# Rotary rows of all attention heads gathered in one tile, in a three-layer model kernel on one core

## The chip, the core and the metric

The kernel runs on one core of one Trainium2 chip. The metric is the device time of one execution in microseconds (us), the median over runs. A core has TensorE (PE in the profile), VectorE (DVE), ScalarE (ACT), GpSimd (POOL) and SyncE (SP), each with its own instruction queue, and 16 DMA engines. SP and ACT issue DMAs here. The engines wait for one another by semaphores alone.

## The reference

Two equal hybrid layers over 512 tokens of width 1024, then a third of another kind. Only the hybrid layer is touched:

```python
def apply_partial_rope(t, cos, sin):            # t: (B, S, 8 heads, 64)
    half = ROPE_DIM // 2                         # 8; ROPE_DIM = 16
    t1 = t[..., :half]
    t2 = t[..., half:ROPE_DIM]
    return jnp.concatenate([t1 * cos - t2 * sin, t2 * cos + t1 * sin, t[..., ROPE_DIM:]], axis=-1)

    h = rms_norm(x, norm_mix_w)
    z = h @ w_in + b_in
    aq, ak, av = ...                             # 8 heads of 64 each, from z
    aq = apply_partial_rope(aq, cos, sin)
    ak = apply_partial_rope(ak, cos, sin)
    ya = dilated_mixture_attention(aq, ak, av)
    yb = ...                                     # mLSTM branch
    x = x + (ga * (ya @ w_proj_att) + gb * (yb @ w_proj_mlstm)) @ w_out
    x = x + jnp.square(jax.nn.relu(rms_norm(x, norm_mlp_w) @ w_ff1)) @ w_ff2
```

So of the 64 rows of a head, 16 are turned and 48 pass through.

## The kernel before

Everything is fp32. A matrix product is three matmuls of split operands (`h_hi` with `w_hi`, `h_lo` with `w_hi`, `h_hi` with `w_lo`), 128x512 each. Activations lie feature-major: the queries and keys of a layer are one tile `qk` of 128 partitions and 8 x 512 columns; a block of 512 columns (one t) holds two heads, on partitions 0 to 63 and 64 to 127, blocks 0 to 3 the queries and 4 to 7 the keys. The rows that turn are partitions 0 to 15 and 64 to 79.

**The weight stream.** Weights come in units of 2048 columns (1 MB). Unit n is loaded by SP into `w_raw` (two slots), copied to `w_hi` by ACT (128x2048), and its remainder written to `w_lo` by POOL in four instructions of 128x512 (L297). SP issues the load of unit n once POOL has split unit n-2, because they share a slot. A unit of the input projection holds 48 matmuls.

**What sets the order.** Each engine's program is the concatenation of stages in one order. While a stage (`rope`, `att`, ...) waits on vector work, PE is given pieces of the input projection (`side`), six matmuls each. A stage gets a budget of pieces in `BESIDE1`: `rope` 18, `att` 36. In `rope` PE does nothing but its pieces. The first score matmul of `att` then waits for `rope.ends`. In `att` the pieces are spread over 19 steps.

**Units of a hybrid layer**, counted from 0: 0 to 3 give `qk`, 4 and 5 the values, 6 to 9 the input of the convolution (`conv_in`). The evacuation of `qk` is one DVE multiplication by `rstd` (L2972) and an ACT bias (L2976). Four units later (`LATER`), just behind the load of units 4 to 7, SP copies the 8-row halves of two blocks crosswise from `qk` to `rope_swapped` (`Rope.move`), so that the last such copies stand behind the load of unit 7. `rope_swapped` has the shape of `qk` and is otherwise zero (a memset by DVE, one for each of the two layers); `cos` is 1 and `sin` 0 in the rows that don't turn (`C_MSK`, `C_UNM`). `Rope.dve` rotates two blocks at a time with three 128x1024 operations, 12 in all, and multiplies the queries by -1/8 on the way.

Of the kernel before, what the change touches and what calls it, by code (L numbers as in the profile page):

```python
# [34 lines left out]
ALU = mybir.AluOpType  # L35
# [50 lines left out]
C_INV = C_PAT + TT * P  # L86
C_MSK, C_UNM = C_INV + 1, C_INV + 2
C_CNT = C_INV + 3
C_SEL = C_CNT + len(WINDOWS) * 16
# [7 lines left out]
def constants():  # L97
    c = np.zeros((P, C_END), np.float32)
    i = np.arange(P)
    c[:, C_ID:C_ID + P] = np.eye(P)  # L100
    c[:, C_ONE:C_ONE + 8] = 1.0
    c[:, C_QK:C_QK + P] = np.where(i[None, :] > i[:, None], BIG, 0.0)
    c[:, C_ST:C_ST + P] = np.where(i[:, None] > i[None, :], BIG, 0.0)
    c[:, C_KEEP:C_KEEP + P] = i[:, None] <= i[None, :]
    for b in range(TT):
        dist = i[:, None] - i[None, :] + (TT - 1 - b) * P
        n = sum(((dist >= 0) & (dist % dil == 0) & (dist <= win)).astype(int) for win, dil in PATTERNS)
        c[:, C_PAT + b * P:C_PAT + (b + 1) * P] = np.where(n > 0, -np.log(np.maximum(n, 1)), BIG)
    d = i % HD
    inv = np.float32(ROPE_THETA) ** (-np.arange(0, ROPE_DIM, 2, dtype=np.float32) / np.float32(ROPE_DIM))  # L110
    half = ROPE_DIM // 2
    c[:, C_INV] = np.where(d < ROPE_DIM, np.where(d < half, -inv[d % half], inv[d % half]), 0.0)
    c[:, C_MSK] = d < ROPE_DIM
    c[:, C_UNM] = d >= ROPE_DIM
    for g, w in enumerate(WINDOWS):
        c[:, C_CNT + 16 * g:C_CNT + 16 * (g + 1)] = 1.0 / np.minimum(np.arange(1, 17), w)
    c[:, C_SEL:C_SEL + SH] = i[:, None] % GROUP == np.arange(SH)[None, :]
    return c


class Stage:
# [55 lines left out]
    def act(self, e): pass  # L177
# [445 lines left out]
class Jobs(Stage):  # L623
# [3 lines left out]

    PIECE, LATER = 6, 4

    def __init__(self, k, name, prev, hand, before):  # L630
        super().__init__(k, name, prev)
        self.units, self.jobs, self.pieces = [], [], []
        self.pos = {"pe": 0, "act": 0, "dve": 0}
        self.joined = set()
        self.early = self.posts = 0
        self.moves = {}
        self.marks, self.marked = [], 0
        self.narrow, self.scale_at = None, None
        self.hand, self.before, self.hooks = hand, before, {}
# [266 lines left out]
class Rope(Stage):  # L906
# [4 lines left out]

    def __init__(self, k, name, prev, qk, swapped):
        super().__init__(k, name, prev)
        self.qk, self.swapped = qk, swapped
        self.ends = [self.at("turned", self.UNITS)]

    def tally(self):
        return {"swapped": 64 * self.UNITS, "cos": self.UNITS, "sin": self.UNITS, "turned": self.UNITS}

    def move(self, j):  # L920
        half, w = ROPE_DIM // 2, slice(2 * j * T, (2 * j + 2) * T)

        def issue(sp):
            for h in (0, HD):
                sp.dma_start(self.swapped[h:h + half, w], self.qk[h + half:h + 2 * half, w])\
                   .then_inc(self.sem("swapped"), 16)
                sp.dma_start(self.swapped[h + half:h + 2 * half, w], self.qk[h:h + half, w])\
                   .then_inc(self.sem("swapped"), 16)
        return issue

    def pe(self, pe):
        self.side_pe(pe, 0, 1)

    def dve(self, dve):
        k = self.k
        self.join(dve)
        both = lambda x: x.unsqueeze(1).broadcast_to([P, 2, T])
        for j in range(self.UNITS):
            self.side_out("dve", dve, 3 * j, 3 * self.UNITS)
            scale = -HD ** -0.5 if j < self.UNITS // 2 else 1.0  # L940
            w = slice(2 * j * T, (2 * j + 2) * T)
            tiles, swapped = (x[:, w].rearrange("p (a b) -> p a b", b=T) for x in (self.qk, self.swapped))
            if j == 0:
                dve.wait_ge(*self.at("swapped", 64 * self.UNITS))
            dve.scalar_tensor_tensor(tiles, tiles, scale, both(k.cos[:, :]), ALU.mult, ALU.mult)\
               .then_inc(self.sem("cos"), 1)
            self.side_out("dve", dve, 3 * j + 1, 3 * self.UNITS)
            dve.scalar_tensor_tensor(swapped, swapped, scale, both(k.sin[:, :]), ALU.mult, ALU.mult)\
               .then_inc(self.sem("sin"), 1)
            self.side_out("dve", dve, 3 * j + 2, 3 * self.UNITS)  # L950
            dve.wait_ge(*self.at("cos", j + 1))
            dve.wait_ge(*self.at("sin", j + 1))
# [1053 lines left out]
class Params(Stage):  # L2006
# [3 lines left out]
    def __init__(self, k, name, sets, norm, at):  # L2010
        super().__init__(k, name, [])
        self.sets, self.norm = sets, norm
        self.prow = [k.at(f"{name}_rows{i}", at + i * P, P) for i in range(len(sets))]
        self.nrow = k.at(f"{name}_norm", at + len(sets) * P, P)
        self.ends = [self.at("cols", 1 + len(sets) + 2 + DEPTH)]

# [18 lines left out]
    def dve(self, dve):  # L2035
# [68 lines left out]
class Setup(Stage):  # L2104
# [131 lines left out]
class Rotary(Stage):  # L2236


    def __init__(self, k, name, prev, angles):
        super().__init__(k, name, prev)  # L2240
        self.rs, self.rc = angles.w[2], angles.w[3]
        self.ends = [self.at("cos", 1)]

    def act(self, act):
# [3 lines left out]
        act.activation(k.cos[:, :], self.rc[:, :], ACT.Sin).then_inc(self.sem("sines"), 1)  # L2248

    def dve(self, dve):  # L2250
        k = self.k
        dve.wait_ge(*self.at("sines", 2))
        dve.tensor_scalar(k.cos[:, :], k.cos[:, :], k.cst[:, C_MSK:C_MSK + 1], k.cst[:, C_UNM:C_UNM + 1],
                          ALU.mult, ALU.add).then_inc(self.sem("cos"), 1)

# [665 lines left out]
def first_layer(k, l, A, st, before, setup, angles, params):  # L2921
# [34 lines left out]
    fill = add(Fill, "fill", [(mv[:, :].rearrange("p (g d) -> p g d", d=MD + 1)[:, :, MD:MD + 1], 1.0),  # L2956
                              (cv3[:, :, 0:CONV - 1], 0.0)] + ([(swapped[:, :], 0.0)] if l else []), prev=[])
    w_in = A["w_in"]
# [15 lines left out]

    def biased(dst, c, bcol, move=None):
        job = scaled(dst, c, lambda act: act.activation(dst, dst, ACT.Identity, bias=k.col(c0 + bcol)))  # L2976
        job.move = move
        return job

# [30 lines left out]
    def gate_out(dve, cols):  # L3010
        for s, n in spread.ends:
# [3 lines left out]
            vb[:, 512:520].unsqueeze(1).broadcast_to([P, TT, 8]), ALU.add)  # L3015
    rope = Rope(k, "rope", [], qk, swapped)
    for j in range(4):
        qk_at = plain(AQ + j * UC, UC, [biased(qk[:, t * T:(t + 1) * T], t, B1 + t, rope.move(j) if t % 2 else None)
                                        for t in (2 * j, 2 * j + 1)])
    side.hooks = {1: [params.turn], 6: [hand.sums], 8: [hand.spread]} if l == 0 else \  # L3020
# [42 lines left out]
    rest = add(Rest, "to_rope", side, max(at, qkv_at), qk_at, prev=[])  # L3063
    rope.prev = [rest, setup, rotary] if l == 0 else [rest]
    rope.settle()
# [266 lines left out]
def program(nc, A, table, out):  # L3332
    with ExitStack() as ctx:
# [55 lines left out]
```

## Time and profile before

| | |
|---|---|
| median of 3 runs | 2417.63 us (2417.51 to 2417.8) |
| the profiled execution's own time | 2417.25 us |
| its span, first to last instruction | 2415.4 us |
| granted TensorE clock, mean | 0.999 |
| PE busy | 2389.6 us, 99% of the span |
| DVE, ACT, POOL busy | 1013.5, 847.4, 1099.3 us (42%, 35%, 46%) |
| DMA moved | 218.27 MB, mean 90 GB/s |

Times in the rows are us from the start of the span. A row in order of time gives start, duration, engine, line and operation, and in brackets how long the engine was idle before it and who ended that. "SPq" and "ACTq" rows are DMA issues. The two hybrid layers show the same pattern, the second 738.60 us after the first at the place of this change; the argument is told for the first.

### The profile page before, as it was taken

The numbers are of one execution on the slowest core, as the hardware profiler recorded it, in microseconds if no ns is written. First come the engines' busy times: TensorE is split into PE (matmuls) and PEld (weight loads), VectorE is DVE, ScalarE is ACT, GpSimd is POOL, SyncE is SP. The second block draws the span as 40 slices with busy tenths as digits, with TensorE's granted clock in tenths as the row PEclk, the third lists the DMA queues.
The fourth block names the chain that finished last, engine by engine and source line by source line (L and its number), as shares of the span: only waits on it lengthen the run. The fifth ranks groups of instructions, "written<-read, shape, count | busy, mean of one in ns | idle before, by whom it ended". The sixth has DMA issues, their size and how long they took to land.

```text
span 2415.4 us, 28668 instructions
## 1 busy us (share of the span) xinstructions
PE 2389.6 (99%) x11096; PEld 1926.8 (80%) x11096; DVE 1013.5 (42%) x1559; ACT 847.4 (35%) x1045; POOL 1099.3 (46%) x796
## 2 busy tenths in 40 slices
PE   8999999999999999999999999999999999999998
PEld 7767888888888767888888888778786788888887
DVE  7657553201203557554211203668595534222202
ACT  5355333322324255233321323442425233322213
POOL 4524355554544533345554544352342345455542
PEclk9999999999999999999999999999999999999999
DMA  5212232223223222222223232221221222322221
GB/s 184 91 53 88 71 103 92 100 88 104 88 104 98 90 70 88 80 94 88 93 99 104 87 105 89 89 73 59 77 88 53 81 99 88 104 91 100 89 103 69
DMA packets 168837, 218.27 MB, mean 90 GB/s; under 512 B 8044, under 2 KB 143148, under 8 KB 168484
## 3 DMA queue, kind: packets, MB, share of 16 engines
q1 hardware_dynamic: 165988, 211.38, 26.5%
q10 hardware_dynamic: 2752, 5.52, 0.7%
q8 instruction: 70, 1.15, 0.2%
q14 instruction: 27, 0.22, 0.0%
HBM read 213.24 MB, written 2.11 MB: 89 GB/s over the span
## 4 chain that ended last, share of the span: by engine, by line
issue 47%; POOL 32%; PE 20%; POOLq 0%; DMA 0%; ACT 0%; DVE 0%; SPq 0%
POOL w_lo L297 32%; PE ps L338 4%; PE ps L336 4%; PE ps L337 4%; PE ps L856 3%; PE ps L1951 2%; PE ps L1953 2%; PE ps L1949 2%; DMA w_raw<-in_w_in 0%; POOLq L308 0%; PE ps L356 0%; PE ps L326 0%; PE ps L362 0%; PE ps L329 0%; PE ps L325 0%
## 5 line engine op out<-in xcount | busy, mean ns | idle before, releaser
L297 POOL TENSOR_TENSOR w_lo<-w_raw,w_hi 128x512 fp32r<-128x512 f32 x792 | 1099.1, 1419 | 1289.6 <-ACT w_hi L283 1279.9
L283 ACT ACTIVATE w_hi<-w_raw 128x2048 fp32r<-128x2048 f32 x197 | 377.4, 1916 | 1044.8 <-PE ps L338 393.7
L856 PE MATMUL ps<-h_hi,w_hi 128*128 128x512 f32 x912 | 370.1, 406 | 4.5 <-POOL w_lo L297 2.9
L856 PE MATMUL ps<-h_hi,w_lo 128*128 128x512 f32 x912 | 356.5, 391 | 0.0
L856 PE MATMUL ps<-h_lo,w_hi 128*128 128x512 f32 x912 | 355.7, 390 | 0.0
L336 PE MATMUL ps<-h_hi,w_hi 128*128 128x512 f32 x816 | 319.4, 391 | 0.0
L338 PE MATMUL ps<-h_hi,w_lo 128*128 128x512 f32 x816 | 318.0, 390 | 0.0
L337 PE MATMUL ps<-h_lo,w_hi 128*128 128x512 f32 x816 | 317.8, 389 | 0.0
L856 PEld LDWEIGHTS ps<-h_hi,w_hi 128*128 128x128 f32 x912 | 171.5, 188 | 46.4 <-issue 8.2
L856 PEld LDWEIGHTS ps<-h_hi,w_lo 128*128 128x128 f32 x912 | 171.3, 188 | 37.0
L856 PEld LDWEIGHTS ps<-h_lo,w_hi 128*128 128x128 f32 x912 | 171.8, 188 | 35.8 <-issue 2.1
L1951 PE MATMUL ps<-ff_lo,w_hi 128*128 (+1 forms) x512 | 199.4, 390 | 0.0
L1953 PE MATMUL ps<-ff_hi,w_lo 128*128 (+1 forms) x512 | 199.4, 390 | 0.0
L1949 PE MATMUL ps<-ff_hi,w_hi 128*128 (+1 forms) x512 | 199.4, 389 | 0.0
L337 PEld LDWEIGHTS ps<-h_lo,w_hi 128*128 128x128 f32 x816 | 153.3, 188 | 32.5 <-issue 0.7
L336 PEld LDWEIGHTS ps<-h_hi,w_hi 128*128 128x128 f32 x816 | 153.3, 188 | 32.1 <-issue 0.7
L338 PEld LDWEIGHTS ps<-h_hi,w_lo 128*128 128x128 f32 x816 | 153.3, 188 | 31.7
L1999 DVE TENSOR_TENSOR xT<-xT,ps 128x512 f32<-128x512 f32 x40 | 27.5, 688 | 346.4 <-PE ps L1953 345.9
L1949 PEld LDWEIGHTS ps<-ff_hi,w_hi 128*128 128x128 f32 x512 | 96.2, 188 | 20.0
L1951 PEld LDWEIGHTS ps<-ff_lo,w_hi 128*128 128x128 f32 x512 | 96.2, 188 | 19.9
L1953 PEld LDWEIGHTS ps<-ff_hi,w_lo 128*128 128x128 f32 x512 | 96.2, 188 | 19.7
L1812 DVE SCALAR_TENSOR_TENSOR ff_relu<-ps,rstd 128x1024 f32<-128x1024 f32 x32 | 39.2, 1225 | 165.9 <-PE ps L338 157.9
(419 smaller groups left out, 3511.7 us busy)
## 6 DMA issues: line engine op xcount, KB each, us to landing
w_raw<-in_w_in SPq DMA_DIRECT2D x71, 1024.0 KB, 4.8
w_raw<-in_w_ff SPq DMA_DIRECT2D x64, 1024.0 KB, 5.1
w_raw<-in_w_ffn_in SPq DMA_DIRECT2D x22, 1024.0 KB, 4.9
w_raw<-in_w_out SPq DMA_DIRECT2D x12, 1024.0 KB, 5.1
w_raw<-in_w_ffn_out SPq DMA_DIRECT2D x11, 1024.0 KB, 4.7
w_raw<-in_w_proj_att SPq DMA_DIRECT2D x4, 1024.0 KB, 4.8
w_raw<-in_w_proj_mlstm SPq DMA_DIRECT2D x4, 1024.0 KB, 4.8
w_raw<-in_w_up_ssd SPq DMA_DIRECT2D x4, 1024.0 KB, 4.6
```

What stands on the lines that cost most here:

```text
L283: act.activation(k.whi[:, slot * SLOT:(slot + 1) * SLOT], k.wraw[:, slot * SLOT:(slot + 1) * SLOT], ACT.Copy).then_inc(k.hi_done, CHUNKS)
L297: pool.tensor_tensor(k.wlo[:, a:a + T], k.wraw[:, a:a + T], k.whi[:, a:a + T], ALU.subtract)\
L336: pe.matmul(out, k.whi[:, w], xh(i), start=i == 0, stop=False)
L337: pe.matmul(out, k.whi[:, w], xl(i), start=False, stop=False)
L338: mm = pe.matmul(out, k.wlo[:, w], xh(i), start=False, stop=i == kt - 1)
L856: mm = pe.matmul(out, lhs, rhs, start=i == 0 and n == 0, stop=stop and n == 2)
L1812: dve.scalar_tensor_tensor(r.rearrange("p (a b) -> p a b", b=T), k.ps[:, 2 * j:2 * j + 2, :], 0.0, rstd, ALU.max, ALU.mult).then_inc(self. ...
L1949: pe.matmul(k.ps[:, c, :], k.whi[:, w], self.fhi[:, x], start=first and i == 0, stop=False, skip_group_check=True)
L1951: pe.matmul(k.ps[:, c, :], k.whi[:, w], self.flo[:, x], start=False, stop=False, skip_group_check=True)
L1953: mm = pe.matmul(k.ps[:, c, :], k.wlo[:, w], self.fhi[:, x], start=False, stop=last and i == 1, skip_group_check=True)
L1999: dve.tensor_tensor(x, x, k.ps[:, c, :], ALU.add).then_inc(self.sem("added"), 1)
```

## The change

The rows that turn, 16 of each of 8 blocks and both halves, are gathered in one tile `rope_turning` of 128 partitions and 1024 columns (row group h, j at partition (h/64 x 4 + j) x 16), their crosswise copy in `rope_swapped` of the same shape. Three DVE operations rotate all of it. Eight transfers of 16 rows and 64 KB put the result back into `qk`: four for the lower half issued by ACT, four for the upper half issued by SP directly behind its load of unit 9 (`UNITS_AHEAD`). `rope.ends` is now the landing of all eight. Each group of copies behind a load grows from four transfers to six. The factor -1/8 moves into the evacuation of the queries, which becomes a scalar_tensor_tensor, with its bias scaled once in the setup (two 128x4 operations). Both memsets of `rope_swapped` and the masking of `cos` go. The budgets become 10 and 44 pieces.

```diff
-            self.side_out("dve", dve, 3 * j, 3 * self.UNITS)
-            scale = -HD ** -0.5 if j < self.UNITS // 2 else 1.0
...
-            dve.scalar_tensor_tensor(tiles, tiles, scale, both(k.cos[:, :]), ALU.mult, ALU.mult)\
...
-            dve.scalar_tensor_tensor(swapped, swapped, scale, both(k.sin[:, :]), ALU.mult, ALU.mult)\
...
-            dve.tensor_tensor(tiles, tiles, swapped, ALU.add).then_inc(self.sem("turned"), 1)
+        self.side_out("dve", dve, 0, 4)
+        dve.wait_ge(*self.at("gathered", 96 * self.UNITS))
+        dve.tensor_tensor(turning, turning, both(k.cos[:, :]), ALU.mult).then_inc(self.sem("products"), 1)
+        dve.tensor_tensor(swapped, swapped, both(k.sin[:, :]), ALU.mult).then_inc(self.sem("products"), 1)
+        dve.wait_ge(*self.at("products", 2))
+        dve.tensor_tensor(turning, turning, swapped, ALU.add).then_inc(self.sem("turned"), 1)
...
     def act(self, act):
+        self.back(act, 0)
         self.side_out("act", act, 1, 1)
...
+    def back(self, eng, h):
+
+        eng.wait_ge(*self.at("turned", 1))
+        for j in range(self.UNITS):
+            a = self.rows(h, j)
+            eng.dma_start(self.qk[h:h + ROPE_DIM, 2 * j * T:(2 * j + 2) * T], self.turning[a:a + ROPE_DIM, :])\
+               .then_inc(self.sem("back"), 16)
...
+            if self.turned and n == self.UNITS_AHEAD:
+                self.turned.back(sp, HD)
...
-        self.ends = [self.at("turned", self.UNITS)]
+        self.ends = [self.at("back", 32 * self.UNITS)]
...
-BESIDE1 = {"turn": 2, "forget": 5, "gates": 9, "rope": 18, "att": 36, "conv": 16, "mlstm": 56}
+BESIDE1 = {"turn": 2, "forget": 5, "gates": 9, "rope": 10, "att": 44, "conv": 16, "mlstm": 56}
...
-        dve.memset(self.swapped, 0.0)
...
+        return Job("dve", lambda dve, bank: dve.scalar_tensor_tensor(
+            dst, k.ps[:, bank, :], -HD ** -0.5, rstd, ALU.mult, ALU.mult), c=t % UT,
```

The DMA queue of SP in the first layer. Before, from the last copies of `qk` (behind unit 7's load) to the following loads; `unit_split` is POOL's semaphore, `side_post` that of ACT's bias:

```order
L266 DMA w_raw<-in_w_in 128x8x256 [waits unit_split]
L925 DMA rope_swapped<-qk 8x1024 [waits side_post]
L927 DMA rope_swapped<-qk 8x1024
L925 DMA rope_swapped<-qk 8x1024
L927 DMA rope_swapped<-qk 8x1024
L266 DMA w_raw<-in_w_in 128x8x256 [waits unit_split] x2
L266 DMA w_raw<-in_w_in 128x4x512 [waits unit_split] x2
```

The same place of the change:

```order
L263 DMA w_raw<-in_w_in 128x8x256 [waits unit_split]
L931 DMA rope_turning<-qk 16x1024 [waits side_post]
L933 DMA rope_swapped<-qk 8x1024
L935 DMA rope_swapped<-qk 8x1024
L931 DMA rope_turning<-qk 16x1024
L933 DMA rope_swapped<-qk 8x1024
L935 DMA rope_swapped<-qk 8x1024
L263 DMA w_raw<-in_w_in 128x8x256 [waits unit_split] x2
L944 DMA qk<-rope_turning 16x1024 [waits rope_turned]
L944 DMA qk<-rope_turning 16x1024 x3
L263 DMA w_raw<-in_w_in 128x4x512 [waits unit_split] x2
```

Six copies stand where four stood, and four transfers back have come between the loads of units 9 and 10.

ACT in the same stretch, around the `w_hi` copy of unit 7 (`unit_landed_1`), before:

```order
L1349 ACTIVATE gate_cols<-ps 128x16 [waits decay_cols]
L283 ACTIVATE w_hi<-w_raw 128x2048 [waits unit_used,unit_landed_1]
L2976 ACTIVATE conv_in<-conv_in,all_param_cols 128x512 [waits side_bank1]
L283 ACTIVATE w_hi<-w_raw 128x2048 [waits unit_used,unit_landed_0]
L2976 ACTIVATE conv_in<-conv_in,all_param_cols 128x512 [waits side_bank2]
```

and of the change:

```order
L1357 ACTIVATE gate_cols<-ps 128x16 [waits decay_cols]
L280 ACTIVATE w_hi<-w_raw 128x2048 [waits unit_used,unit_landed_1]
L944 DMA qk<-rope_turning 16x1024 [waits rope_turned]
L944 DMA qk<-rope_turning 16x1024 x3
L2976 ACTIVATE conv_in<-conv_in,all_param_cols 128x512 [waits side_bank1]
L280 ACTIVATE w_hi<-w_raw 128x2048 [waits unit_used,unit_landed_0]
```

The transfers of the lower half stand between unit 7's `w_hi` copy and the next bias.

PE, the end of the pieces and the first scores of `att`, before:

```order
L856 MATMUL ps<-h_hi,w_hi 128x512
L856 MATMUL ps<-h_lo,w_hi 128x512
L856 MATMUL ps<-h_hi,w_lo 128x512
L1047 MATMUL ps<-qk 128x128 [waits side_bank2,side_bank1,side_bank3,side_bank0,side_post,decay_emt,rope_turned]
L1047 MATMUL ps<-qk 128x128
```

and of the change:

```order
L855 MATMUL ps<-h_hi,w_hi 128x512
L855 MATMUL ps<-h_lo,w_hi 128x512
L855 MATMUL ps<-h_hi,w_lo 128x512
L1055 MATMUL ps<-qk 128x128 [waits side_bank2,side_bank1,side_bank3,side_bank0,side_post,decay_emt,rope_back]
L1055 MATMUL ps<-qk 128x128
```

The first scores have moved up by 48 matmuls (eight pieces), and their last wait is for the transfers instead of the DVE. The multiset of PE's instructions is the same.

## Rows read from the trace of the kernel before

**Rows 1.** The page, part 1: engine, busy us, share, instructions.

```profile
PE 2389.6 (99%) x11096; PEld 1926.8 (80%) x11096; DVE 1013.5 (42%) x1559; ACT 847.4 (35%) x1045; POOL 1099.3 (46%) x796
```

**Rows 2.** Waits of PE: who, us in total, times, longest.

```profile
PE ps L856 <- POOL w_lo L297: 3.7, 4, 1.2
```

**Rows 3.** Order of time, PE, end of unit 6 and start of unit 7.

```profile
95.91 0.39 PE L856 MATMUL ps<-h_hi,w_lo 128*128 128x512 f32 x1
97.52 0.50 PE L856 MATMUL ps<-h_hi,w_hi 128*128 128x512 f32 x1 [1.22 <-POOL w_lo L297]
```

**Rows 4.** The same place in the second layer.

```profile
836.12 0.50 PE L856 MATMUL ps<-h_hi,w_hi 128*128 128x512 f32 x1 [1.22 <-POOL w_lo L297]
```

**Rows 5.** PE, first and last of the 108 matmuls of the stage, and the first scores.

```profile
85.12 0.50 PE L856 MATMUL ps<-h_hi,w_hi 128*128 128x512 f32 x1
...
111.04 0.39 PE L856 MATMUL ps<-h_hi,w_lo 128*128 128x512 f32 x1
111.36 0.49 PE L1047 MATMUL ps<-qk 64*128 64x128 f32 x4
```

**Rows 6.** POOL in order of time: units 6 and 7, and unit 7 of the second layer.

```profile
79.01 5.02 POOL L297 TENSOR_TENSOR w_lo<-w_raw,w_hi 128x512 fp32r<-128x512 f32 x4 [12.81 <-ACT w_hi L283]
88.85 8.62 POOL L297 TENSOR_TENSOR w_lo<-w_raw,w_hi 128x512 fp32r<-128x512 f32 x4 [4.81 <-ACT w_hi L283]
...
827.44 8.62 POOL L297 TENSOR_TENSOR w_lo<-w_raw,w_hi 128x512 fp32r<-128x512 f32 x4 [5.06 <-ACT w_hi L283]
```

**Rows 7.** DVE in order of time, start of the rotation.

```profile
87.29 1.22 DVE L945 SCALAR_TENSOR_TENSOR qk<-qk,cos 128x1024 f32<-128x1024 f32 x1
88.42 1.22 DVE L948 SCALAR_TENSOR_TENSOR rope_swapped<-rope_swapped,sin 128x1024 f32<-128x1024 f32 x1
89.75 2.12 DVE L953 TENSOR_TENSOR qk<-qk,rope_swapped 128x1024 f32<-128x1024 f32 x1
91.80 0.68 DVE L2972 TENSOR_TENSOR conv_in<-ps,rstd 128x512 f32<-128x512 f32 x1
```

**Rows 8.** Order of time, around the two memsets.

```profile
1.70 3.47 DVE L2154 MEMSET rope_swapped<- 128x4096 f32 x1 [0.82 <-issue]
...
4.91 0.27 PE L2019 MATMUL ps<-constants,all_params_norm 8*128 8x8 f32 x1 [4.91 <-DMA all_params_norm<-in_norm_mix_w]
...
770.90 0.69 DVE L2972 TENSOR_TENSOR qk<-ps,rstd 128x512 f32<-128x512 f32 x1 [0.82 <-ACT rstd L454]
```

**Rows 9.** SP's issues: unit 7 and the copies behind it, then unit 9.

```profile
66.23 0.37 SPq L266 DMA_DIRECT2D w_raw<-in_w_in  x1
...
68.66 0.62 SPq L927 DMA_DIRECT2D rope_swapped<-qk  x1
...
97.49 0.37 SPq L266 DMA_DIRECT2D w_raw<-in_w_in  x1
```

**Rows 10.** Stretches: engines' busy us (instructions), PE clock, DMA share, GB/s.

```profile
66.20:70.45 4.25, 4.25 (x21) 3.50 (x20) 1.77 (x11) 1.71 (x3) 0.00 (x1) 1.00 0.75 226
70.45:71.65 1.20, 1.20 (x9) 0.87 (x8) 0.00 (x0) 0.00 (x0) 0.00 (x0) 1.00 0.51 181
71.65:72.65 1.00, 1.00 (x10) 0.82 (x8) 0.20 (x1) 0.00 (x0) 0.00 (x0) 1.00 0.00 0
```

**Rows 11.** DMA queue from 39.55 to 42.35, four copies alone: packets, MB, share.

```profile
q1 hardware_dynamic: 64, 0.13, 31.4%
```

**Rows 12.** A 16-row transfer of ACT's queue: us to landing; and ACT's next copy.

```profile
s_rows<-s_rows ACTq DMA_DIRECT2D x3, 32.0 KB, 2.0
...
96.42 1.91 ACT L283 ACTIVATE w_hi<-w_raw 128x2048 fp32r<-128x2048 f32 x1 [3.18 <-PE ps L856]
```

**Rows 13.** PE's last matmuls, and the granted clock in stretches after.

```profile
2406.92 2.82 PE L2794 MATMUL ps<-constants,xT 128*128 128x128 f32 x24
...
2409.00:2412.40 3.40, 0.74 (x7) 0.50 (x5) 1.53 (x3) 1.16 (x3) 0.00 (x0) 1.00 0.89 365
2412.50:2415.40 2.90, 0.00 (x0) 0.00 (x0) 0.00 (x0) 0.00 (x0) 0.00 (x0) 0.50 0.68 277
```

More of the change, by code:

```diff
@@ L86 @@
 C_INV = C_PAT + TT * P
-C_MSK, C_UNM = C_INV + 1, C_INV + 2
-C_CNT = C_INV + 3
+C_CNT = C_INV + 1
 C_SEL = C_CNT + len(WINDOWS) * 16
@@ L108, in constants @@
         c[:, C_PAT + b * P:C_PAT + (b + 1) * P] = np.where(n > 0, -np.log(np.maximum(n, 1)), BIG)
-    d = i % HD
+    d = i % ROPE_DIM
     inv = np.float32(ROPE_THETA) ** (-np.arange(0, ROPE_DIM, 2, dtype=np.float32) / np.float32(ROPE_DIM))
     half = ROPE_DIM // 2
-    c[:, C_INV] = np.where(d < ROPE_DIM, np.where(d < half, -inv[d % half], inv[d % half]), 0.0)
-    c[:, C_MSK] = d < ROPE_DIM
-    c[:, C_UNM] = d >= ROPE_DIM
+    c[:, C_INV] = np.where(d < half, -inv[d % half], inv[d % half])
     for g, w in enumerate(WINDOWS):
@@ L637, in __init__ @@
         self.marks, self.marked = [], 0
-        self.narrow, self.scale_at = None, None
+        self.narrow, self.scale_at, self.turned = None, None, None
         self.hand, self.before, self.hooks = hand, before, {}
@@ L910, with __init__, rows @@
     UNITS = 4
-    def __init__(self, k, name, prev, qk, swapped):
+    def __init__(self, k, name, prev, qk, at):
         super().__init__(k, name, prev)
-        self.qk, self.swapped = qk, swapped
-        self.ends = [self.at("turned", self.UNITS)]
+        self.qk = qk
+        self.turning, self.swapped = (k.at(f"rope_{n}", at + i * 2 * T, 2 * T)
+                                      for i, n in enumerate(("turning", "swapped")))
+        self.ends = [self.at("back", 32 * self.UNITS)]
     def tally(self):
-        return {"swapped": 64 * self.UNITS, "cos": self.UNITS, "sin": self.UNITS, "turned": self.UNITS}
+        return {"gathered": 96 * self.UNITS, "products": 2, "turned": 1, "back": 32 * self.UNITS}
+    def rows(self, h, j):
+        return (h // HD * self.UNITS + j) * ROPE_DIM
     def move(self, j):
@@ L924, in issue @@
             for h in (0, HD):
[L925 to L928, printed above, removed]
-        return issue
+                a = self.rows(h, j)
+                sp.dma_start(self.turning[a:a + ROPE_DIM, :], self.qk[h:h + ROPE_DIM, w])\
+                  .then_inc(self.sem("gathered"), 16)
+                sp.dma_start(self.swapped[a:a + half, :], self.qk[h + half:h + 2 * half, w])\
+                  .then_inc(self.sem("gathered"), 16)
+                sp.dma_start(self.swapped[a + half:a + 2 * half, :], self.qk[h:h + half, w])\
+                  .then_inc(self.sem("gathered"), 16)
+        return issue
+    def back(self, eng, h):
+        eng.wait_ge(*self.at("turned", 1))
+        for j in range(self.UNITS):
+            a = self.rows(h, j)
+            eng.dma_start(self.qk[h:h + ROPE_DIM, 2 * j * T:(2 * j + 2) * T], self.turning[a:a + ROPE_DIM, :])\
+               .then_inc(self.sem("back"), 16)
     def pe(self, pe):
@@ L937, in dve @@
         both = lambda x: x.unsqueeze(1).broadcast_to([P, 2, T])
[L938 to L953 removed]
+        turning, swapped = (x[:, :].rearrange("p (a b) -> p a b", b=T) for x in (self.turning, self.swapped))
+        self.side_out("dve", dve, 0, 4)
[4 more added lines that the diff above has]
+        dve.tensor_tensor(turning, turning, swapped, ALU.add).then_inc(self.sem("turned"), 1)
         self.side_out("dve", dve, 1, 1)
     def act(self, act):
+        self.back(act, 0)
         self.side_out("act", act, 1, 1)
@@ L2014, in __init__ @@
         self.nrow = k.at(f"{name}_norm", at + len(sets) * P, P)
-        self.ends = [self.at("cols", 1 + len(sets) + 2 + DEPTH)]
+        self.ends = [self.at("cols", 1 + len(sets) + 2 + 2 * DEPTH)]
     def turn_norm(self, pe):
@@ L2048, in dve @@
                .then_inc(self.sem("cols"), 1)
+            dve.tensor_scalar(k.qbias[:, l * 4:l * 4 + 4], k.pall[:, l * NPC + B1:l * NPC + B1 + 4], -HD ** -0.5, None,
+                              ALU.mult).then_inc(self.sem("cols"), 1)
 class Loads(Stage):
@@ L2241, in __init__ @@
         self.rs, self.rc = angles.w[2], angles.w[3]
-        self.ends = [self.at("cos", 1)]
+        self.ends = [self.at("sines", 2)]
     def act(self, act):
@@ L2973, in scaled, with biased, turned @@
         return Job("dve", evac, c=c % UT, post=post)
[L2975 to L2978, printed above, removed]
+    def biased(dst, c, bcol):
+        return scaled(dst, c, lambda act: act.activation(dst, dst, ACT.Identity, bias=k.col(c0 + bcol)))
+    def turned(j, t):
+        dst, move = qk[:, t * T:(t + 1) * T], rope.move(j) if t % 2 else None
+        if t >= KD // 2:
+            job = biased(dst, t, B1 + t)
+            job.move = move
+            return job
+        bias = k.qbias[:, l * 4 + t:l * 4 + t + 1]
+        return Job("dve", lambda dve, bank: dve.scalar_tensor_tensor(
+            dst, k.ps[:, bank, :], -HD ** -0.5, rstd, ALU.mult, ALU.mult), c=t % UT,
+            post=lambda act: act.activation(dst, dst, ACT.Identity, bias=bias), move=move)
     def wide(c0, job):
@@ L3015, in gate_out @@
             vb[:, 512:520].unsqueeze(1).broadcast_to([P, TT, 8]), ALU.add)
-    rope = Rope(k, "rope", [], qk, swapped)
+    rope = Rope(k, "rope", [], qk, o_ya)
+    side.turned = rope
     for j in range(4):
-        qk_at = plain(AQ + j * UC, UC, [biased(qk[:, t * T:(t + 1) * T], t, B1 + t, rope.move(j) if t % 2 else None)
-                                        for t in (2 * j, 2 * j + 1)])
+        qk_at = plain(AQ + j * UC, UC, [turned(j, t) for t in (2 * j, 2 * j + 1)])
     side.hooks = {1: [params.turn], 6: [hand.sums], 8: [hand.spread]} if l == 0 else \
@@ L3348, in program @@
         k.hbias = k.keep("half_bias", DEPTH * 20)
+        k.qbias = k.keep("query_bias", DEPTH * 4)
         k.small = k.keep("small", 48)
```

14 lines of the change are left out of this document (3 added, 11 removed).

## The prediction

> **What bounds the kernel now.** I read the shares of the engines first: PE is busy 2389.6 of 2415.4 us [rows 1], and the change leaves PE's instructions as they are. So DVE work saved is worth nothing by itself; what counts is where PE stands still. Next the waits of PE. All its waits for `w_lo` together are 3.7 us in four places [rows 2], and in order of time two of the four, 1.22 us each, stand inside this rotation, one in each layer [rows 3, 4]. The reader is to see there that PE ends unit 6 and finds unit 7 not split. Why is it late? POOL's four instructions take 5.02 us for unit 6 and 8.62 us for unit 7 [rows 6], and beside unit 7 DVE runs the rotation, whose 128x1024 operations themselves stretch from 1.22 to 2.12 us there [rows 7]. So these two engines slow each other, and PE pays 1.22 us for it. Around it, PE runs 108 matmuls from 85.12 to the first scores at 111.36 [rows 5]; the DVE rotation before is what those 18 pieces cover.
>
> **The change, part by part.** All times are in the first layer; the second repeats them.
>
> *The stall that goes.* The 48 matmuls of unit 6 start between 85.12 and 95.91, a step of 10.79 / 47 = 0.23 [rows 3, 5]. Unit 7 could start at 96.14 and started at 97.52: 1.38 us lost. After the change the rotation is three operations instead of twelve. In the trace the first three are done at 89.75 + 2.12 = 91.87 [rows 7], with the same sizes and the same neighbour, so I take 91.9 for `turned` (their copies have landed long before: two more issues of 0.62 in a group whose data were in by 71.65 [rows 9, 10]). POOL's 8.62 us hold 3.60 us of stretching over four instructions [rows 6]; the rotation now lies beside two of them, so I keep half: 88.85 + 5.02 + 1.8 = 95.7. That is 0.4 us before PE's 96.14. The stall goes: -1.38 us per layer, if POOL keeps that margin.
>
> *The scores move up.* 60 matmuls instead of 108 stand before them. Unit 7 gives 12: the last starts at 96.14 + 11 x 0.23 = 98.7, and the scores follow 0.32 later, as 111.36 follows 111.04 [rows 5]: PE is ready at 99.0.
>
> *The lower half's transfers back.* ACT issues four of them from 91.9. At 0.62 an issue [rows 9] the last starts at 93.8, and 16-row transfers of ACT's queue land after 2.0 us [rows 12]; even with 0.5 more for twice the bytes that is 96.3, hidden behind the pieces by 2.7 us. What queues behind them on ACT is a bias and, at 96.42, unit 8's `w_hi` copy [rows 12]; the issues end at 94.4. Nothing.
>
> *The upper half's transfers back.* They are issued behind the load of unit 9, which SP issues the moment POOL ends unit 7: 97.49 against 88.85 + 8.62 = 97.47 [rows 6, 9]. Now that is 95.7, and `turned` is met by then. The trace shows how such a group fares. Unit 7's load is issued at 66.23, four small copies behind it until 68.66 + 0.62 [rows 9]; the queue is busy with the load at a share of 0.75 until about 70.45, works on for another 1.2 us at 0.51, and is still at 71.65 [rows 10]. So the small transfers wait for the megabyte in front of them: their data begin about 4.3 us after the load's issue, and all is in 5.4 after it. Those copies were 8 rows, 32 KB, on four different row groups. The transfers back are 64 KB each, 256 KB, all four into the same 16 rows. Their tail is the unknown:
> - lower bound, as the copies behind a load, the whole group landing 5.4 after the issue: 101.1;
> - nearest row: four copies alone, when their packets do move together, keep the queue at a share of 31.4% for 2.80 us with 32 packets of data [rows 11], that is 0.314 x 16 x 2.80 / 32 = 0.44 us a packet. With four packets behind one another on each of 16 engines the tail is 1.8 us: 95.7 + 4.3 + 1.8 = 101.8;
> - upper bound, 16 rows at once twice as slow per packet as 8: tail 3.5, 103.5.
>
> I take the middle one, since the four transfers aim at one set of rows, and 0.1 for the hand-over: the scores start at 101.9 instead of 99.0. PE waits 2.9 us.
>
> A rule of the Trainium skill bears on it (SBUF — State Buffer, "Door 1: The DMA port swizzle"): 16 rows reach only 4 of the 16 DMA ports, about 109 GB/s. By it the 256 KB take 2.4 us and land at 102.4, and the sum below would be 1.2 us more. By it the median would be 2421.8. No row here shows a queue of such transfers, so it stays out of the sum.
>
> *What costs nothing.* The first memset of `rope_swapped` ends at 5.17, and the next DVE work needs a PE result of 5.18; behind the second one DVE waited for ACT anyway [rows 8]. The `cos` mask, the bias scaling and the new form of the query evacuation lie on DVE, which PE waits for nowhere near them. SP's two more issues per group cost 1.3 us, and SP then waits for POOL before the next load in any case. In `att` 44 pieces instead of 36 give each softmax step more cover, not less.
>
> *Sum.* Per layer -1.38 + 2.9 = +1.5, for two layers +3.0: 2417.25 + 3.0 = 2420.3 for the profiled execution, which is 0.4 under the median of the runs. So 2420.6 as a median, +0.12%. One measurement of this kernel can tell about 0.2%, 4.8 us, from no change; the forecast is "no change that can be told, on the slow side".
>
> **Rivals.**
> - *The transfers are hidden.* If SP's land by 99.0, only the gain stays: -2.8, 2414.9. For it: the DMA engines are idle but for the load, and 256 KB is little. Against it: the copies behind a load never came in less than 5.4 us after it, and here only 3.3 us are there. It takes a queue that doesn't keep order.
> - *A slow tail (the other side).* Slower than before by more than 4.8 us if the wait goes over 3.8 us in each layer, that is if the tail is over 2.7 us. At the upper bound the scores start at 103.6: wait 4.6, +3.2 per layer, 2424.0. For it: all four go to the same rows while the load's last packets still move. Against it: it doubles the nearest row.
> - *TensorE's clock falls in the wait (also beyond 0.2%, if in both layers).* PE ends at 2406.92 + 2.82 = 2409.74; the granted clock is 1.00 until 2412.40 and 0.50 from 2412.50 [rows 13]: it fell to the 1.2 GHz level some 2.7 us after the last matmul. A wait of 2.9 us is as long. If the level then stays low for about as long as the wait (no row shows how long), half of 2.9 is lost: +1.5 in one layer, 2422.1; in both, 2423.6. Against it: the 1.22 us stalls left the clock at 0.999 on average, and 2.9 is barely over 2.7. The Trainium skill (TensorE: Matmul & The Clock Gate, "Why this matters for your kernels") names idle gaps between bursts of matmuls as what brings the lower level; the end of this trace agrees, and no row here shows a gap of that length inside the kernel.
> - *The stall stays.* If POOL ends unit 7 0.5 us later than I think, at 96.2, hardly any stall is left, but the load, and with it the transfers, come 0.5 later: +1.0 for two layers, 2421.6. It is inside the forecast's own range.
>
> **How the numbers follow.** The forecast with its own bounds (landing between 101.1 and 102.6, 2419.2 to 2422.3): 0.57. Hidden or nearly: 0.10, of which faster by over 0.2% next to nothing. Slow tail: 0.13. Clock: 0.15, of which two thirds end over 2422.5. Something I don't see: 0.05, both signs. The predicted time is the forecast's, 2420.6. Leaving out the ends of the rivals, the range is 2416.5 to 2424.0. Slower by over 0.2%: 0.13 + 0.10 + 0.02 = 0.25; faster: 0.02; within: 0.73.
>
> **What would show it.** In the profile after: no wait of PE for `w_lo` in the two rotations, POOL's unit 7 in about 6.8 us; DVE some 39 us less busy (nine operations fewer per layer at some 1.7, between the 1.22 and 2.12 of [rows 7], and two memsets of 3.47); a new wait of the first score matmul for a DMA `qk<-rope_turning`, near 3 us, twice; the transfers' data begin after the load of unit 9 in SP's queue. Wrong if that wait is missing or over 3.8 us, if the clock row shows 0.5 behind it, if POOL still ends after 96.1, or if the span moves while these waits don't.

## The result: 2428.3 us, 0.43% slower, and the profile after

| | before | after |
|---|---|---|
| median, 6 runs each | 2417.59 us (2417.33 to 2419.20) | 2428.28 us (2427.30 to 2429.18) |
| ratio | | 1.0043, 95% interval 1.0033 to 1.0053 |
| profiled execution: own time, span | 2417.25, 2415.4 us | 2428.61, 2426.8 us |
| granted clock, mean | 0.999 | 0.997 |

The forecast was 2420.6, the range 2416.5 to 2424.0. The side was right ("on the slow side"), the size was not: 10.7 us are lost instead of 3.0, and the time lies 4.3 us above the range. In the kernel before and in several versions below, some executions take about 1.5 us more than the rest with the same mean clock (14 of the 70 of the kernel before that were timed beside the experiments), so a difference of less than that between single executions isn't read as an effect.

The page's span and busy times, after:

```profile
span 2426.8 us, 28672 instructions
PE 2395.0 (99%) x11096; PEld 1929.4 (80%) x11096; DVE 977.4 (40%) x1540; ACT 847.6 (35%) x1045; POOL 1088.9 (45%) x796
```

Against [rows 1] DVE works 36 us less, and PE, with the same matmuls, shows 5.4 us more busy time. An engine that takes longer for the same instructions is the first sign of a slower clock. PE's waits:

```profile
PE ps L1055 <- DMA qk<-rope_turning: 8.4, 2, 4.2
...
PE ps L855 <- POOL w_lo L294: 1.3, 2, 0.8
```

The two long waits for `w_lo` of [rows 2] are gone (3.7 us in four places have become 1.3 in two), and a wait of the scores for the transfers back has come, 4.2 us in each layer. The first layer by engine in order of time, DVE, POOL, ACT, SP and PE one behind the other (start, duration, engine, line; in brackets the idle time before it and who ended it):

```profile
87.67 1.22 DVE L957 TENSOR_TENSOR rope_turning<-rope_turning,cos 128x1024 f32<-128x1024 f32 x1
88.80 1.22 DVE L958 TENSOR_TENSOR rope_swapped<-rope_swapped,sin 128x1024 f32<-128x1024 f32 x1
90.05 2.19 DVE L960 TENSOR_TENSOR rope_turning<-rope_turning,rope_swapped 128x1024 f32<-128x1024 f32 x1
...
89.22 6.68 POOL L294 TENSOR_TENSOR w_lo<-w_raw,w_hi 128x512 fp32r<-128x512 f32 x4 [4.80 <-ACT w_hi L280]
...
92.28 2.54 ACTq L944 DMA_DIRECT2D qk<-rope_turning  x4
...
95.93 0.37 SPq L263 DMA_DIRECT2D w_raw<-in_w_in  x1
96.35 2.48 SPq L944 DMA_DIRECT2D qk<-rope_turning  x4
...
99.00 0.39 PE L855 MATMUL ps<-h_hi,w_lo 128*128 128x512 f32 x1
103.57 0.80 PE L1055 MATMUL ps<-qk 64*128 64x128 f32 x4 [4.18 <-DMA qk<-rope_turning]
```

The work of this layer stands some 0.37 us later than before (the first piece at 85.49, before 85.12 [rows 5]), a shift from the start of the program that differs from one profile to the next by some tenths. PE's last piece starts at 99.00, and without a wait the score would start 0.32 later, at 99.32; it starts at 103.57, 4.25 us late. `x4` at 0.80 us is the second sign: in a version without a wait (below) the same four take 0.49. The clock, in the windows around its two changes (each line: window, its length, busy time and starts of PE, PEld, DVE, ACT and POOL, then granted clock, DMA share, GB/s):

```profile
99.23:102.72 3.49, 0.16 (x1) 0.00 (x0) 0.00 (x0) 0.09 (x1) 3.49 (x4) 1.00 0.81 225
102.72:109.55 6.83, 5.98 (x16) 4.30 (x16) 0.51 (x4) 0.88 (x4) 1.00 (x1) 0.50 0.48 156
109.55:114.00 4.45, 4.45 (x21) 2.78 (x20) 1.98 (x8) 1.71 (x5) 0.00 (x0) 1.00 0.00 0
...
846.83:853.66 6.83, 6.00 (x16) 4.30 (x16) 0.51 (x4) 0.88 (x4) 0.95 (x1) 0.50 0.47 154
```

The granted clock falls to the 1.2 GHz level at 102.72, still inside the wait, and stays there for 6.83 us, 5.98 of them with PE at work. The second layer repeats it. Before, the clock fell only behind PE's last matmul [rows 13].

### The profile page after: what moved, and what is told of

Same layout as the page of the kernel before. It is cut to its first block, busy times and chain, and to the rows that moved or that the text cites. A ratio compares the mean times of both kernels' runs of the same rounds, so it can differ in the third digit from the quotient of the medians.

```text
span 2426.8 us, 28672 instructions
## 1 busy us (share of the span) xinstructions
PE 2395.0 (99%) x11096; PEld 1929.4 (80%) x11096; DVE 977.4 (40%) x1540; ACT 847.6 (35%) x1045; POOL 1088.9 (45%) x796
## 3 DMA queue, kind: packets, MB, share of 16 engines
q10 hardware_dynamic: 3008, 6.05, 0.8%
## 4 chain that ended last, share of the span: by engine, by line
issue 48%; POOL 31%; PE 20%; POOLq 0%; ACT 0%; DMA 0%; DVE 0%; SPq 0%
POOL w_lo L294 31%; PE ps L334 4%; PE ps L333 4%; PE ps L335 4%; PE ps L855 3%; PE ps L1959 2%; PE ps L1957 2%; PE ps L1961 2%; POOLq L305 0%; PE ps L2136 0%; DMA all_params_norm<-in_norm_mix_w 0%; PE ps L326 0%; PE ps L323 0%; PE ps L353 0%; PE ps L352 0%
```

## Where 10.7 us come from

The first score and the next group of scores (`64x256`) have the same work between them here and in the version without a wait (`e1_before_load`), 16 matmuls. Here they start at 103.57 and 109.67, 6.10 us apart; there at 99.40 and 102.77, 3.37 apart. The second layers give the same two numbers. The low level costs 2.73 us a layer. So a layer changes by -1.38 (the stall that is gone) + 4.25 (wait) + 2.73 (clock) = +5.6, two by 11.2; the two profiled executions differ by 11.4, the medians by 10.7.

The wait itself, from the single packets and the semaphore events of the trace (no view prints them): SP's load of unit 9, issued at 95.93, moves from 96.96 to 100.88; the 64 packets of 4 KB behind it from 100.43 to 102.66, 0.31 us each on average; their last semaphore write is done at 102.69; the score starts 0.88 after that. In the trace the semaphore `back` rises for the last time at 103.53, 0.84 after that write, and the score follows 0.04 later. So this time lies between the packet and the rise, not in PE. ACT's four, issued 4 us earlier, are in by 96.18.

## The experiments

Each is timed beside the kernel before, on the same chip as it (medians of before 2417.46, 2417.64 and 2417.71 in the three groups, 2417.59 beside the change). `e7_dve_load` starts from `e1_before_load` and `e9_load_waits` from `e8_all_act`; the others change one thing of the kernel after.

### e1_before_load: SP's transfers ahead of the load

```diff
-    PIECE, LATER, UNITS_AHEAD = 6, 4, 9
+    PIECE, LATER, UNITS_AHEAD = 6, 4, 8
```

> The change with SP's four transfers back issued ahead of the load of unit 9 instead of behind it. Theory (the cost is the place behind the load, and the clock falls in the wait that comes of it): the four are issued from 92.3 like ACT's and land by about 96.5, before PE is ready at 99.0; no wait of the first score, no row of the clock at 0.5 in the two rotations, growth of a layer -1.38 in place of +5.5: 2428.3 - 2 x 6.9 = 2414.5, at most 2415.5. Rival (part of the loss lies elsewhere, in the 44 pieces beside the attention or in the evacuation): over 2417. Rival (transfers back are slow wherever they stand): a wait of the first score for a DMA stays, over 1 us.

Measured: 2414.48 us (2414.28 to 2415.95), 0.9988 of before, interval 0.9979 to 0.9997. SP and PE:

```profile
92.35 2.45 SPq L944 DMA_DIRECT2D qk<-rope_turning  x4
96.00 0.37 SPq L263 DMA_DIRECT2D w_raw<-in_w_in  x1
...
99.08 0.39 PE L855 MATMUL ps<-h_hi,w_lo 128*128 128x512 f32 x1
99.40 0.49 PE L1055 MATMUL ps<-qk 64*128 64x128 f32 x4
```

The score follows the last piece after 0.32, no stretch of 0.50 is left inside the program, and the load isn't later than it was (96.00 against 95.93), because SP had been waiting for POOL there. One number moved, and 13.8 us come back, as the theory said. The kernel is now a little faster than before.

### e2_budget18: the old cover

```diff
-BESIDE1 = {"turn": 2, "forget": 5, "gates": 9, "rope": 10, "att": 44, "conv": 16, "mlstm": 56}
+BESIDE1 = {"turn": 2, "forget": 5, "gates": 9, "rope": 18, "att": 36, "conv": 16, "mlstm": 56}
```

> The change with the budgets of before, 18 pieces in the rotation and 36 beside the attention; the transfers stay behind the load. Theory: PE has 48 matmuls more, 10.9 us, ahead of the first score and is ready at about 110, transfers landed at 102.7 cost nothing: no wait, no fall of the clock, 2414.5 to 2415.5. Rival (the transfers' traffic or the evacuation costs PE time by itself, wait or not): over 2417.

Measured: 2414.41 us (2414.23 to 2414.75), 0.9987 (0.9978 to 0.9996). The transfers stand as late as in the change; PE comes later:

```profile
96.16 2.48 SPq L944 DMA_DIRECT2D qk<-rope_turning  x4
...
109.71 0.39 PE L855 MATMUL ps<-h_hi,w_lo 128*128 128x512 f32 x1
110.03 0.49 PE L1055 MATMUL ps<-qk 64*128 64x128 f32 x4
```

So the rest of the change costs nothing, and the same 3 us are won as in `e1_before_load`: the loss is the wait and what follows it alone. Either repair beats both kernels, by 0.12 to 0.13% against the one before.

### e3_both_halves: SP's four transfers on two sets of rows

SP calls `back` with 2 and ACT with 0.

```diff
-    def back(self, eng, h):
+    def back(self, eng, j0):
...
-        for j in range(self.UNITS):
-            a = self.rows(h, j)
-            eng.dma_start(self.qk[h:h + ROPE_DIM, 2 * j * T:(2 * j + 2) * T], self.turning[a:a + ROPE_DIM, :])\
-               .then_inc(self.sem("back"), 16)
+        for j in (j0, j0 + 1):
+            for h in (0, HD):
+                a = self.rows(h, j)
+                eng.dma_start(self.qk[h:h + ROPE_DIM, 2 * j * T:(2 * j + 2) * T], self.turning[a:a + ROPE_DIM, :])\
+                   .then_inc(self.sem("back"), 16)
```

> The change with the eight transfers shared out otherwise: each queue writes the lower and the upper 16 rows of two pairs of blocks, so SP's four go to two sets of rows instead of one. Theory A (the tail is set by the rows that four transfers share): packets of SP's group go down from 0.31 us mean, the tail from 2.26 to about 1.2, wait 3.2 in place of 4.25; if the clock still falls, 2426; if it doesn't, 2421. Theory B (the tail is set by the packets' own time and the load in front, whatever rows): 2428.3 within 0.5.

Measured: 2425.61 us (2423.03 to 2426.10, 7 runs). SP's 64 packets take 0.22 us instead of 0.31 on average; all is in 1.64 us after the first of them begins (100.35 to 101.99), where the change needs 2.26. In the second layer it is 1.94 against 2.46, and the other profiles in which four transfers to one set of rows stand behind the load have 2.1 to 2.9. Theory A holds in its kind; of the tail 0.5 to 0.6 us belongs to the shared rows, not the 1.1 expected. The first score:

```profile
102.68 0.80 PE L1056 MATMUL ps<-qk 64*128 64x128 f32 x4 [3.38 <-DMA qk<-rope_turning]
```

and the window in which the clock is low:

```profile
102.51:105.92 3.41, 3.24 (x10) 2.53 (x11) 0.51 (x4) 0.88 (x4) 1.12 (x1) 0.50 0.30 67
```

A wait shorter by 0.8 us, and a low level of 3.41 us instead of 6.83, which costs 1.5 us instead of 2.7 (the next group of scores starts 4.84 us after the first). The profiled execution is one of the faster ones; how long the level was low in the others isn't on record.

### e4_budget12, e5_budget11, e10_budget8: how long a wait brings the low level

They are the edit of `e2_budget18` with 12 and 42, 11 and 43, 8 and 46 in place of 18 and 36. The transfers land as in the change; PE is ready later or earlier.

> The change with 12 pieces in the rotation and 42 beside the attention: PE is ready 2 x 6 x 0.227 = 2.72 us later, at 101.7, the transfers land as before, the first score at 103.57: wait about 1.5 in place of 4.25. Theory (a wait under the 2.7 us that the clock took to fall at the end of the program leaves it at 1.00): no row of 0.5 in the rotations, 2428.3 - 2 x (2.7 + 2.6) = 2417.7. Rival (any wait of that kind brings the lower level): 0.5 for some us behind it, 2421 to 2423.

> The change with 11 pieces in the rotation and 43 beside the attention: PE is ready 1.36 us later than with 10, so the wait is about 2.9, the one that the prediction had for the change itself. Theory (a wait of 2.9 is long enough for the clock in most executions; with 1.7 it fell in some): median 2423 to 2426, executions spread by some us, mean clock 0.997 to 0.998. Rival (the clock holds up to some 3 us): all executions within 0.5 of 2420.6, the forecast, with a clock of 0.999 to 1.000.

> The change with 8 pieces in the rotation and 46 beside the attention: PE is ready 2.7 us earlier, the transfers land as before, the wait is about 7. Theory (the low clock costs a fixed piece of work behind any wait that brings it, some 6.8 us at half speed): 2428.3 + 2 x 2.7 = 2433.7, the rows at 0.5 as long as in the change. Rival (the loss grows with the wait): rows at 0.5 of 10 us and more, 2436 or over.

Measured, with the mean clock that each execution was granted:

| pieces | step to the first score, each layer | median (lowest to highest) | single executions |
|---|---|---|---|
| 12 | 2.08, 1.92 | 2419.60 (2417.47 to 2423.05) | five at 2417.5 to 2418.3, clock 0.999 to 1.000; four at 2419.6 to 2421.0, 0.998 to 0.999; two at 2423.0, 0.997 |
| 11 | 3.89, 3.19 | 2425.21 (2420.36 to 2426.89) | 2420.4 and 2420.9 with 0.999; nine from 2423.9 on with 0.997 to 0.998 |
| 10 (the change) | 4.57, 4.60 | 2428.28 (2427.30 to 2429.18) | all with 0.996 to 0.998 |
| 8 | 7.45, 7.63 | 2434.42 (2432.60 to 2434.92) | all with 0.995 to 0.997 |

The windows of one execution each. With 12 pieces, behind the first wait:

```profile
103.80:110.00 6.20, 6.20 (x29) 4.58 (x30) 1.84 (x11) 1.98 (x8) 0.00 (x0) 1.00 0.53 172
```

With 11, the low stretches of the two rotations, and a third one elsewhere:

```profile
104.35:107.76 3.41, 3.41 (x11) 2.61 (x12) 0.51 (x4) 0.88 (x4) 0.00 (x0) 0.50 0.83 271
845.04:851.87 6.83, 6.14 (x16) 4.30 (x16) 1.21 (x5) 1.60 (x5) 0.89 (x1) 0.50 0.47 154
1640.35:1643.76 3.41, 3.41 (x11) 2.73 (x10) 2.83 (x4) 0.00 (x0) 2.71 (x2) 0.50 0.00 0
```

With 8, the low stretch cut at the first score, and what follows it:

```profile
99.51:103.70 4.19, 0.00 (x1) 0.00 (x1) 0.00 (x0) 0.00 (x0) 4.15 (x4) 0.50 0.59 147
103.70:109.75 6.05, 6.05 (x16) 4.30 (x16) 0.51 (x4) 0.88 (x4) 0.00 (x0) 0.50 0.53 173
109.75:112.00 2.25, 2.25 (x12) 1.58 (x12) 1.34 (x7) 0.96 (x4) 0.00 (x0) 1.00 0.00 0
```

With 12 pieces my theory fell in its plain form: a wait of 1.7 us leaves the clock alone in the profiled execution (2418.06, expected 2417.7), but not in every one: the two executions at 2423.0 and the two of the middle four with 0.998 show a fall in their mean clock. The other two of the four, 2419.6 and 2419.8 with 0.999, need not be falls, since other versions have such executions without one. In the profiled executions the waits are 1.8 and 1.6 us with 12 pieces and 3.6 and 2.9 with 11 (the step less 0.32); those of the others aren't on record. So at waits of about 1.6 to 3.6 us whether the clock falls differs from one execution to the next, and it falls more often with the longer ones; with 4.2 and more the mean clock shows a fall in every execution. In `e8_all_act` below, with 2.9 and 3.1, all seven executions lie 2.7 us or more above the 2420.4 that the two waits alone would give (2414.5 + 6.0).

With 11 pieces the two executions with the clock up took 2420.4 and 2420.9: that fits the forecast's own case, waits of about 3 us without a fall, and its time was 2420.6.

With 8 pieces the level is low for 10.24 us, as the rival had it, but 4.19 of them lie in the wait, where they cost nothing; 6.05 us of work stay, as in the change, and the time is 0.7 over the theory's 2433.7 and 1.6 under the rival's. What the clock costs doesn't grow further with the wait; the wait itself still costs its own length.

### e6_idle_filled: matmuls of no use in the wait

```diff
     def pe(self, pe):
         self.side_pe(pe, 0, 1)
+        for _ in range(17):
+            pe.matmul(self.k.ps[:, 4, :], self.k.hhi[:, 0:P], self.k.hhi[:, 0:T], start=True, stop=True)
```

> The change with 17 more matmuls of 128x512, of no use, behind the pieces of each rotation (2 x 3.9 us of PE work whose results nobody reads), so that PE is busy until just before the transfers land. Theory (the low clock behind the wait costs 2.6 to 2.9 us a layer and comes from PE's standing still): the first score starts at 103.6 to 103.8 as in the change, no row at 0.5, 2428.3 - 2 x 2.75 = 2422.8, within 0.7. Rival (the clock falls for another reason, such as the small matmuls of the attention): 2428.3 and the rows at 0.5 stay. The rows also show whether the 0.9 us from the last packet to the first score belong to an engine that stood still (then 0.3 here) or to the transfer (then 0.9 stays).

Measured: 2423.87 us (2423.18 to 2425.32, 8 runs), 4.4 under the change; expected were 5.5, the highest executions being 2 us over the lowest. PE:

```profile
101.72 1.29 PE L950 MATMUL ps<-h_hi 128*128 128x512 f32 x5
103.61 0.49 PE L1057 MATMUL ps<-qk 64*128 64x128 f32 x4 [0.59 <-DMA qk<-rope_turning]
```

and the window behind the first score:

```profile
103.61:109.55 5.94, 5.94 (x28) 4.38 (x29) 2.49 (x12) 2.59 (x9) 0.00 (x0) 1.00 0.56 179
```

Useless work makes the kernel faster: the score starts no earlier (103.61 against 103.57), but 28 instead of 16 matmuls start in the same 6 us. It shows that the low level behind this wait comes of PE's standing still. And the time between the last packet (102.59) and the score is 1.02 us although PE had been at work until 0.6 us before: it isn't an engine that has to wake. The semaphore's last rise stands at 103.56, so 0.97 of the 1.02 us pass before PE can know of the landing.

### e7_dve_load: three more DVE operations beside POOL

It starts from `e1_before_load`; the count of `products` goes from 2 to 5 with it.

```diff
         dve.tensor_tensor(turning, turning, swapped, ALU.add).then_inc(self.sem("turned"), 1)
+        for i in range(3):
+            dve.wait_ge(*self.at("turned", 1) if i == 0 else self.at("products", 2 + i))
+            dve.tensor_tensor(swapped, swapped, both(k.sin[:, :]), ALU.mult).then_inc(self.sem("products"), 1)
```

> The version with SP's transfers ahead of the load, and three more operations of 128x1024 on DVE right behind the rotation (rope_swapped by sin again, whose result nobody reads), some 5.5 us in which DVE works beside POOL's split of unit 7 as it did before. Theory (the 1.38 us are won because nine operations fewer stand beside POOL's split): POOL's unit 7 goes back from 6.7 to 8.6 us, a wait for w_lo of about 1.2 returns in each layer, 2414.5 + 2 x 1.3 = 2417.1. Rival (the stall went for another reason, such as the start of POOL's work): no such wait, 2414.5.

Measured: 2417.51 us (2417.37 to 2419.25), 0.9999 of before (0.9990 to 1.0008). POOL, DVE and PE:

```profile
89.05 8.61 POOL L294 TENSOR_TENSOR w_lo<-w_raw,w_hi 128x512 fp32r<-128x512 f32 x4 [4.80 <-ACT w_hi L280]
...
92.12 6.63 DVE L963 TENSOR_TENSOR rope_swapped<-rope_swapped,sin 128x1024 f32<-128x1024 f32 x3
...
97.72 0.50 PE L855 MATMUL ps<-h_hi,w_hi 128*128 128x512 f32 x1 [1.19 <-POOL w_lo L294]
```

POOL's unit takes 8.61 us again (8.62 before [rows 6]), the stall of 1.2 is back, and the whole gain of 3.0 us is gone. Its cause is shown: DVE's operations beside the split, each of them at 2.2 us instead of 1.22. The second layer has the same 8.61 and a stall of 1.21.

### e8_all_act and e9_load_waits: another queue, and then the load out of the way

e8, where `stream` no longer issues any transfers back:

```diff
     def act(self, act):
         self.back(act, 0)
+        self.back(act, HD)
```

e9 has in addition, ahead of SP's load of unit 9:

```diff
+            if self.turned and n == self.UNITS_AHEAD:
+                sp.wait_ge(*self.turned.at("back", 32 * self.turned.UNITS))
```

> The change with all eight transfers issued by ACT, none behind SP's load. Theory (the place behind the load is the cost, and a group of eight on one idle queue moves as it is issued): issues from 92.3 at 0.61, the last at 96.6, landed 2.3 to 2.7 later at 98.9 to 99.3, the first score at 99.6 to 100.2 instead of 99.3; no fall of the clock; 2414.5 to 2416.3. Rival (eight transfers queue up on one another, 0.37 us for each of 8 packets an engine): landed at 100.5 or later, wait over 1.5, and over 2417.

> The version with all eight transfers issued by ACT, and SP holds the load of unit 9 back until all eight have landed. It tells apart why eight transfers on ACT's own queue came in at 101.3, seven of the eight packets of an engine long after they were issued. Theory (they shared the DMA engines with the load of unit 9, whose packets move from 96.8 on; the queue that they stand in doesn't matter): without the load beside them the last, issued at 96.5, lands at 98.8 to 99.3, the first score starts at 99.6 to 100.2, the clock stays at 1.00, and the load, 3 us later, is still early for unit 9: 2414.4 to 2416.3. Rival (a queue takes eight such transfers no faster): landed at 100.5 or later, over 2417.

Measured: 2424.86 us (2423.15 to 2425.26, 7 runs) and 2414.77 us (2414.48 to 2416.16). In order of time, e8:

```profile
92.03 5.10 ACTq L944 DMA_DIRECT2D qk<-rope_turning  x8
...
101.99 0.49 PE L1056 MATMUL ps<-qk 64*128 64x128 f32 x4 [2.85 <-DMA qk<-rope_turning]
```

and e9:

```profile
99.05 0.37 SPq L263 DMA_DIRECT2D w_raw<-in_w_in  x1
...
98.95 0.39 PE L855 MATMUL ps<-h_hi,w_lo 128*128 128x512 f32 x1
99.27 0.49 PE L1056 MATMUL ps<-qk 64*128 64x128 f32 x4
```

The view of the DMAs gives the median time from issue to landing at a row's end; e8, of the one transfer issued after 96.8:

```profile
qk<-rope_turning ACTq DMA_DIRECT2D x1, 64.0 KB, 5.4
```

e9, of all eight:

```profile
qk<-rope_turning ACTq DMA_DIRECT2D x8, 64.0 KB, 2.4
```

With e8 my theory fell: the transfers stand behind no load in their queue, and yet the last are in only at 101.29. The load's data move from 96.79 to 101.50. Of the 128 packets 96 have started by 96.90; no other starts until 99.58, and the last 32, the bytes of two transfers, start from then to 100.90. In the second layer the same pause lasts from 836.94 to 839.53. e9 holds that load back, and there is no such pause: the last packet is in at 98.69, issued as before, and the score follows PE's pieces without a wait. So it isn't the place in SP's queue, or not that alone: a transfer whose packets come to the DMA engines after a megabyte has started on them is held up by it in the other queue too, for some 2.7 us here, though not until the load is done. The load 3 us later costs 0.3 us against `e1_before_load` at most, within the spread of both. The place in SP's queue decided that all four came after, and e8, where only the last two did, is 3.4 us faster than the change.

## Why the prediction was wrong

Two of its own signs of being wrong came: a wait over 3.8 us, and a clock row at 0.50 behind it. Point by point, by its own steps:

- **The stall that goes: right.** -1.38 a layer predicted; `e7_dve_load` against `e1_before_load` gives 3.03 / 2 = 1.5. POOL's unit 7 takes 6.68 us, 6.85 were forecast (95.7 - 88.85), `turned` is met at 92.24, forecast 91.9 plus the shift of 0.37.
- **PE ready, ACT's transfers, what costs nothing: right.** 99.32 with the shift, forecast 99.0; ACT's in by 96.2, forecast 96.3. `e2_budget18` shows the rest at nothing. The 39 us of DVE work that it names as a sign are 37.5 by its own terms (18 x 1.7 + 2 x 3.47); 36.1 were measured.
- **SP's transfers wait for the load: right as a time, narrower as a reason.** Their data begin 4.5 us after the load's issue, forecast 4.3. The prediction put it down to the queue's order; `e8_all_act` shows a delay of the same kind across queues.
- **The tail: mis-sized.** "With four packets behind one another on each of 16 engines the tail is 1.8 us": 2.26 measured, 2.46 in the second layer. The 0.44 us a packet came from copies of 8 rows; here a packet takes only 0.31, but 64 x 0.31 / 16 = 1.24 us of 2.26, so the packets of an engine don't stand close behind one another, as the step had them. `e3_both_halves` shows 0.5 to 0.6 us of the tail to be the price of one set of rows for all four. The estimate that the prediction set aside, by the Trainium skill (SBUF — State Buffer, "Door 1: The DMA port swizzle"), 2.4 us for 256 KB through 16 rows, was nearer, and the trace agrees with it within 0.14 us.
- **The hand-over: the step that failed first.** "0.1 for the hand-over" had no row behind it. 0.88 and 0.84 us passed from the last packet to the first score, in other versions about 0.7 to 1.2, nearly all of it before the semaphore's last rise. The tail (0.5 too small) and the hand-over (0.8) make up nearly all of the step from 2.9 to 4.25.
- **The clock: the step that failed most.** It was a rival with 0.15, priced at "half of 2.9". At this wait it came in every execution and cost 2.73 us, because the level stays low for some 6 us of work, with a wait of 4.2 as with one of 7. Of the 10.7 us lost, 5.5 are this term. [rows 13] showed a fall 2.7 us after the last matmul but not how long it lasts; the bound from above should have been open there, not the wait's own length.
- **The two rivals were taken as separate.** "Slow tail" (2424.0) and "clock" (2423.6) each alone ended at the range's edge. A slow tail makes the wait longer and with it the fall more likely, so they belong together: the slow tail's wait of 4.6 and half of it for the clock, the prediction's own numbers, would have given 2417.6 + 2 x (-1.38 + 4.6 + 2.3) = 2428.6. That this lands on the measured time is partly luck: its wait is 0.35 too long and its clock 0.43 too cheap.

With the measured sizes the sum is 2417.25 + 2 x (-1.38 + 4.25 + 2.73) = 2428.5 for the profiled execution, which took 2428.61.

## What to carry to other kernels

A small transfer that something waits for should reach the DMA engines before a large load does. Here another queue alone won 3.4 of 13.8 us, an issue four microseconds earlier all of them. Before matmuls are taken from in front of a wait, look at all that they cover: here the old 18 pieces would have hidden the new transfers too, and keeping them was worth as much as the better order. A wait of PE of the lengths seen here, from 1.6 us on, is priced with the clock behind it, here up to 2.8 us each, and two rivals that lengthen the same wait are one case.

## What the runs showed of the hardware that was not expected

- The low level of TensorE's clock lasted 3.41, 6.83 or 10.24 us in these profiles, with at most 6.14 us of PE's work in it. Waits of nearly the same length had different prices: 2.9 us brought none in the first layer of `e8_all_act` and 6.83 us in the second of `e5_budget11`; 3.5 and 3.7 in `e3_both_halves` brought 3.41. The step to the next group of scores grew by about 1.5 us with 3.41 and by 2.7 to 2.8 with 6.83 or 10.24.
- The 2.7 us of [rows 13] is one value of many: at the ends of the twelve profiles the level falls 2.5 to 3.7 us after PE's last matmul, and in the waits 2.1 us after it at the earliest (second layer of `e5_budget11`). In the second layer of `e3_both_halves` it fell only at 846.62, 1.66 us after the first score had started.
- In `e5_budget11` it also fell once at 1640.35, where PE's longest idle time near it is 1.1 us, as in the profiles in which it stayed up there. What brought it stays open. The kernel before, too, has one execution of 70 at 2420.87 with a mean clock of 0.998.
- From the last packet of a group of transfers to the waiting matmul about 0.7 to 1.2 us pass. In every profile with such a wait the matmul starts 0.04 us after the semaphore's last rise; the rest lies between the last packet and that rise, 0.65 to 1.12 us beside or behind the load, and 0.35 and 0.45 in `e9_load_waits`, where no load moves. What fills it was not tried.
